# Wider attention units: as many heads as two PSUM banks take, and a unit's transposes issued together

## The chip, the cores and the metric

The kernel runs on one core of one Trainium2 chip. The metric is the device time of one execution in microseconds (us), and the number compared is the median of several runs. A profiled execution is a further one, whose trace the profile is made of. TensorE (PE) multiplies matrices, VectorE (DVE) and ScalarE (ACT) work on rows, GpSimd (POOL) does a few small steps, and SyncE (SP) starts the transfers. Each engine takes its instructions strictly in program order and waits on semaphores for the others.

## What is computed

Two transformer blocks over 512 tokens of width 1024. The first has eight-head attention under a top-k mask, a retention branch and a feed-forward part; the second has native sparse attention (a compressed, a selected and a window branch), gated linear attention and a feed-forward part with a convolution. What matters here is the softmax attention, of which the first block holds one and the second two (selected "s" and window "w"), each with 8 heads of 64:

```python
# first block: one attention, keys chosen by a mask
logits = jnp.einsum('bqhd,bqkhd->bqhk', qb, kg).astype(jnp.float32) * att_scale
logits = jnp.where(valid[:, :, None, :], logits, NEG)
p = jax.nn.softmax(logits, axis=-1).astype(v.dtype)
return jnp.einsum('bqhk,bqkhd->bqhd', p, vg)

# second block: the compressed branch, then two more whose outputs are gated and added
s_cmp = jnp.einsum('bsghd,bngd->bghsn', q, k_cmp)
p_cmp = masked_softmax(s_cmp, cmp_end[None, :] <= pos[:, None])
o_cmp = jnp.einsum('bghsn,bngd->bsghd', p_cmp.astype(dt), v_cmp).reshape(B, S, NSA_HEADS, D)
```

## The kernel before

The 512 tokens are four tiles of 128. The weight products ("dense" here) make up most of the program: every weight is split into a high and a low part (tiles `wh`, `wl`), the activations too (`Hh`, `Hl`), and three matmuls make one product. The loop over a stage's weight chunks and tiles advances in **ticks**; most ticks are six dense matmuls. Class `Weave` runs other work between the ticks: a generator registered with `w.beside(side, every)` goes on by one step, up to its next `yield`, after every tick or every second one. All engines run the same schedule of ticks and yields, each issuing its own part, so the order on each engine is fixed when the program is built. ScalarE and VectorE also split the coming weights (L1176, L1680) in that order.

Attention is such a generator, once per engine. The first block's (`att1`) runs beside the stages `gr0` and `gr1`, one step every second tick; the second block's (`att2`) beside `2nq`, `2gv` and `2gqk`, one step every tick. Its **units** are two heads each: `(i, hp, br)` is query tile i (0 to 3), head pair hp and branch br. Tile i looks at (i+1) x 128 keys. `att1` has 16 units, `att2` 32. One unit passes through four parts, spread over steps u to u+3:

- **scores** (PE, L539): for each of the two heads a product with 64 rows of contraction, q against (i+1) x 128 keys, the first head into bank 4 and the second into bank 5. The two heads lie on rows 0 to 63 and 64 to 127.
- **max** (DVE, L2001): adds the mask and takes the row's extreme, from PSUM into SBUF; **exp** (ACT, L1348) with the row sum; **scale** (DVE, L1708 reciprocal, L1695 `tensor_scalar`), one step later.
- **turn** (PE, L548): i+1 transposes for each head, into bank 6 for the first and bank 3 for the second; ACT copies them out (L1355).
- **values** (PE, L539): for each key block and head a product of 64 columns, accumulated in bank 7 for the whole tile.

In step u TensorE issues: turn of the first head of unit u-2, scores of unit u, turn of the second head of u-2, values of u-3. Scores wait until max of the unit before has read banks 4 and 5. When the last unit of a tile has gone, `att2` adds the compressed branch (eight products, tile `PCT`), for which the generator yields until that branch is ready, and bank 7 is read out.

Beside it in the second block runs `compressed()`, which for each tile makes eight small score products in the same banks 4 and 5 (operands `PRMT`, `ACC`), whose results DVE must read (tile `PRMT`, L1692) before the banks can be used again; transposes of queries and of the linear branch run there too, and `linear()` follows once attention has ended.

Of the kernel before, what the change touches and what calls it, by code (L numbers as in the profile page):

```python
# [5 lines left out]
S, D, P, T = 512, 1024, 128, 4  # L6
# [303 lines left out]
def program(nc, x_in, cst_in, prm_in, bc_in, brow_in, wst, out):  # L310
# [12 lines left out]
    with ctx:  # L323
# [136 lines left out]
        LEAST, SUMS = ST[:, 592:600], ST[:, 600:608]  # L460
# [53 lines left out]
        class Attention:  # L514


            def __init__(self, tag, branches, scr, pt, sbanks, tbanks):
                self.tag, self.scr, self.pt, self.sbanks, self.tbanks = tag, scr, pt, sbanks, tbanks

                self.units = [(i, hp, br) for i in range(T) for hp in range(4) for br in branches]  # L520
                self.first, self.last = branches[0], branches[-1]

# [6 lines left out]
        def tensor_program(e, on):  # L529
# [254 lines left out]
            def attention(a, query, key, value, ready, vready, extra=None):  # L784
                n = len(a.units)

                def turn_part(u, j):
                    i, p = a.units[u][0], 2 * u + j
                    b, src = a.tbanks[p % len(a.tbanks)], a.scr[p % len(a.scr)]
                    turn(b, [src[:, tok(kb)] for kb in range(i + 1)], dve.of((a.tag, "scaled", p)), (a.tag, "turned", p))  # L790
                    free[b] = act.of((a.tag, "pT", p))

                def scores(u):
                    i, hp, br = a.units[u]
                    for r in ready(i, br):
                        on.wait_ge(*r)
                    for b in a.sbanks:
                        claim(b)
                    for j, b in enumerate(a.sbanks):
                        h = 2 * hp + j  # L800
                        mm(bank[b][:, 0:(i + 1) * P], query(i, h), key(br, i, h), True, True).then_inc(*small.mark((a.tag, "score", 2 * u + j)))
                        free[b] = dve.of((a.tag, "max", 2 * u + j))

                def values(u):
                    i, hp, br = a.units[u]
                    first = hp == 0 and br == a.first
# [5 lines left out]
                    for kb in range(i + 1):  # L812
                        for j in (0, 1):
                            o = bank[7][64 * j:64 * j + 64, tok(hp)]
                            x = mm(o, value(br, kb, 2 * hp + j), a.pt[(2 * u + j) % 4][:, tok(kb)], first and kb == 0, False)
                    x.then_inc(*small.mark((a.tag, "value", u)))
                    if hp == 3 and br == a.last:
                        free[7] = dve.of((a.tag, "out", i))

                for u in range(n + 3):  # L820
                    if 2 <= u < n + 2:
                        turn_part(u - 2, 0)
                    if u < n:
                        scores(u)
                    if 2 <= u < n + 2:
                        turn_part(u - 2, 1)
                    if u >= 3:
                        values(u - 3)
                        i, hp, br = a.units[u - 3]
                        if hp == 3 and br == a.last and extra:  # L830
                            yield from extra(i)
                    yield

# [332 lines left out]
        def scalar_program(e, on):  # L1166
# [173 lines left out]
            def attention(a, extra=None):  # L1340
                n = len(a.units)

                def exps(u):
                    i = a.units[u][0]
                    for p in (2 * u, 2 * u + 1):
                        sc, q = a.scr[p % len(a.scr)][:, 0:(i + 1) * P], p % 8
                        on.wait_ge(*dve.of((a.tag, "max", p)))
                        e.activation(sc, sc, ACT.Exp, scale=-1.0, bias=LEAST[:, q:q + 1], accum_out=SUMS[:, q:q + 1]).then_inc(*act.mark((a.tag, "exp", p)))  # L1348

                def turn_part(u, j):  # L1350
                    p, m = 2 * u + j, (a.units[u][0] + 1) * P
# [5 lines left out]
                for u in range(n + 3):  # L1357
# [5 lines left out]
                    if u >= 3:  # L1363
                        i, hp, br = a.units[u - 3]
                        if hp == 3 and br == a.last:
# [4 lines left out]
                    yield  # L1370

# [291 lines left out]
        def vector_program(e, on):  # L1663
# [323 lines left out]
            def attention(a, mask, mready, coef, cready, extra=None):  # L1987
                n = len(a.units)

                def scores(u):  # L1990
                    i = a.units[u][0]
                    m = (i + 1) * P
                    for j in (0, 1):
                        p = 2 * u + j
                        sc = a.scr[p % len(a.scr)][:, 0:m]
                        on.wait_ge(*small.of((a.tag, "score", p)))
                        if p >= len(a.scr):
# [3 lines left out]
                        e.tensor_tensor_reduce(out=sc, in0=bank[a.sbanks[j]][:, 0:m], in1=mask(i), scale=-0.125, scalar=-GONE, op0=ADD, op1=MIN,  # L2001
                                               accum_out=LEAST[:, p % 8:p % 8 + 1]).then_inc(*dve.mark((a.tag, "max", p)))

                def scale(u):
                    i, hp, br = a.units[u]
                    on.wait_ge(*act.of((a.tag, "exp", 2 * u + 1)))
                    pair = SUMS[:, 2 * u % 8:2 * u % 8 + 2]
                    recip(pair, pair)
                    own()
                    if coef:  # L2010
                        on.wait_ge(*cready)
                    for j in (0, 1):
                        p = 2 * u + j
                        sc, r = a.scr[p % len(a.scr)][:, 0:(i + 1) * P], SUMS[:, p % 8:p % 8 + 1]
                        ts(sc, sc, r, coef(i, 2 * hp + j, br) if coef else None, MUL, MUL if coef else None, (a.tag, "scaled", p))

                for u in range(n + 3):
# [4 lines left out]
                    if u >= 3:  # L2022
                        i, hp, br = a.units[u - 3]
                        if hp == 3 and br == a.last:
# [4 lines left out]
                    yield  # L2029

# [321 lines left out]
            def second_attention():  # L2352
                yield
                yield from attention(att2, lambda i: C("cm", (3 - i) * P, (i + 1) * P), lambda i: (s_cst2, 16),
                                     lambda i, h, br: gt[:, i, 3 * h + 1 + "sw".index(br):3 * h + 2 + "sw".index(br)], act.of(("gt",)), add_compressed)
# [316 lines left out]
```

## Time and profile before

| | us |
|---|---|
| median of 3 runs | 1606.05 (1603.98 to 1607.24) |
| the profiled execution's own time | 1602.26 |
| its span | 1600.4 |
| PE busy in the span | 1576.0 (98%) |
| DVE busy | 875.0 (55%) |
| ACT busy | 613.2 (38%) |
| DMA queue q1, share of 16 engines | 29.7% |

Rows of the page and of the trace carry the line, the engine, the operation, output <- inputs, the shape and a count. A float32 matmul of scores, values or compressed scores appears as two records, so "x4" in a timeline row of scores is two products; a transpose and a dense matmul are one record each. Matmuls overlap, so a record's duration is longer than its share of the engine; what a group takes is read as the time from its first start to the next group's first start.

### The profile page before, as it was taken

What the parts mean: (1) busy time and instruction counts of PE and PEld (TensorE: products, weight loads), DVE (VectorE), ACT (ScalarE), POOL (GpSimd) and SP (SyncE); (2) the same over time, 40 slices, a digit from 0 to 9 for tenths busy, and PEclk for the clock granted to TensorE, in tenths of its full rate; (3) what the DMA queues carried; (4) which work ended last, traced back from release to release, by engine and by line L of the source; (5) the groups of instructions that cost most, each with busy time, mean ns of one, the idle gap of its engine ahead of it and who ended that gap; (6) DMA issues with size and microseconds to landing.
All of it is one profiled execution on the core that took longest, in us unless ns stands there. A gap on an engine that the chain in (4) does not pass through costs nothing.

```text
span 1600.4 us, 19799 instructions
## 1 busy us (share of the span) xinstructions
PE 1576.0 (98%) x8019; PEld 1257.9 (79%) x8019; DVE 875.0 (55%) x1604; ACT 613.2 (38%) x1068; POOL 44.3 (3%) x82
## 2 busy tenths in 40 slices
PE   7999999999999999999999999999999999999999
PEld 5777887678888888888888886666768988888887
DVE  6679785655365653232333665676357555555432
ACT  4443334542312432222332454566425434343330
POOL 0000000000000000000000101100010000000000
PEclk9999999999999999999999999999999999999999
DMA  9322121146345334322232142110113232223321
GB/s 389 129 79 93 56 77 54 52 163 221 104 171 171 106 138 152 105 93 94 90 106 92 43 166 74 41 54 14 40 53 117 93 106 92 90 82 105 108 77 53
DMA packets 44883, 165.76 MB, mean 104 GB/s; under 512 B 5108, under 2 KB 5236, under 8 KB 43640
## 3 DMA queue, kind: packets, MB, share of 16 engines
q1 hardware_dynamic: 44792, 164.50, 29.7%
q8 instruction: 63, 1.03, 0.3%
q14 instruction: 28, 0.23, 0.0%
HBM read 162.38 MB, written 2.10 MB: 103 GB/s over the span
## 4 chain that ended last, share of the span: by engine, by line
PE 92%; DVE 5%; ACT 2%; issue 1%; POOL 1%; DMA 0%; SPq 0%; DVEq 0%; ACTq 0%
PE bank L539 87%; PE bank L548 4%; DVE AR L1692 1%; DVE wl L1680 1%; POOL ST L2483 0%; DVE G L1699 0%; DVE X L1692 0%; DVE Hl L1692 0%; ACT wh L1176 0%; ACT AR L1199 0%; DVE CST L1692 0%; ACT AR L1187 0%; DMA CST<-in_cst 0%; DVE ST L1702 0%; DVE AR L1699 0%
## 5 line engine op out<-in xcount | busy, mean ns | idle before, releaser
L539 PE MATMUL bank<-wh,Hh 128*128 128x512 f32 (+1 forms) x1008 | 407.6, 404 | 1.9 <-DVE Hl L1692 1.0
L539 PE MATMUL bank<-wh,Hl 128*128 128x512 f32 (+1 forms) x1008 | 391.6, 389 | 0.0
L539 PE MATMUL bank<-wl,Hh 128*128 128x512 f32 (+1 forms) x1008 | 390.9, 388 | 0.0
L1176 ACT ACTIVATE wh<-raw 128x1024 fp32r<-128x1024 f32 (+1 forms) x195 | 203.6, 1047 | 398.2 <-PE bank L539 386.2
L1680 DVE TENSOR_TENSOR wl<-raw,wh 128x1024 fp32r<-128x1024 f32 (+1 forms) x195 | 234.2, 1208 | 137.1 <-ACT wh L1176 136.1
L539 PEld LDWEIGHTS bank<-wh,Hh 128*128 128x128 f32 x1008 | 189.5, 188 | 60.3 <-issue 24.9
L539 PEld LDWEIGHTS bank<-wh,Hl 128*128 128x128 f32 x1008 | 189.4, 188 | 40.0
L539 PEld LDWEIGHTS bank<-wl,Hh 128*128 128x128 f32 x1008 | 189.8, 188 | 33.9
L539 PE MATMUL bank<-Hh,wh 128*128 128x512 f32 (+2 forms) x504 | 190.2, 377 | 1.0 <-DVE AR L1692 0.7
L539 PE MATMUL bank<-Hl,wh 128*128 128x512 f32 (+2 forms) x504 | 189.4, 376 | 0.0
L539 PE MATMUL bank<-Hh,wl 128*128 128x512 f32 (+2 forms) x504 | 189.4, 376 | 0.0
L539 PEld LDWEIGHTS bank<-Hh,wh 128*128 128x128 f32 (+1 forms) x504 | 94.5, 187 | 18.6 <-DVE AR L1692 0.9
L1692 DVE TENSOR_TENSOR Hl<-AR,Hh 128x512 fp32r<-128x512 f32 x68 | 45.8, 689 | 115.5 <-ACT Hh L1459 109.2
L539 PEld LDWEIGHTS bank<-Hh,wl 128*128 128x128 f32 (+1 forms) x504 | 94.5, 187 | 17.7
L539 PEld LDWEIGHTS bank<-Hl,wh 128*128 128x128 f32 (+1 forms) x504 | 94.5, 187 | 17.6 <-issue 0.2
L548 PEld LDWEIGHTS bank<-CST,AR 128*128 128x128 f32 (+1 forms) x545 | 66.3, 144 | 44.9 <-issue 10.9
L548 PE MATMUL bank<-CST,AR 128*128 128x128 f32 (+1 forms) x545 | 88.8, 285 | 12.0 <-DVE AR L1695 9.0
L539 PE MATMUL bank<-Hh,Ah 128*128 128x512 f32 (+1 forms) x272 | 99.4, 365 | 0.5 <-DVE X L1692 0.5
L539 PE MATMUL bank<-Hh,Al 128*128 128x512 f32 (+1 forms) x272 | 99.0, 364 | 0.0
L539 PE MATMUL bank<-Hl,Ah 128*128 128x512 f32 (+1 forms) x272 | 99.0, 364 | 0.0
L1176 ACT ACTIVATE Ah<-raw 128x1024 fp32r<-128x1024 f32 x46 | 48.6, 1058 | 125.5 <-PE bank L539 119.3
L1699 DVE SCALAR_TENSOR_TENSOR AR<-bank,PRMT,AR 128x511 f32<-128x511 f32 x88 | 63.8, 746 | 56.2 <-ACT AR L1655 54.7
(249 smaller groups left out, 1851.4 us busy)
## 6 DMA issues: line engine op xcount, KB each, us to landing
raw<-in_wst SPq DMA_DIRECT2D x268, 512.0 KB, 3.6
AR<-in_wst SPq DMA_DIRECT2D x8, 1024.0 KB, 11.0
X<-in_x SPq DMA_DIRECT2D x8, 512.0 KB, 4.5
AR<-in_wst SPq DMA_DIRECT2D x5, 512.0 KB, 5.5
out<-X SPq DMA_DIRECT2D x8, 256.0 KB, 2.1
CST<-in_cst SPq DMA_DIRECT2D x1, 1619.0 KB, 11.8
raw<-in_wst SPq DMA_DIRECT2D x4, 296.0 KB, 2.7
BC<-in_bc SPq DMA_DIRECT2D x2, 512.0 KB, 8.2
```

Source lines behind the costliest of these rows:

```text
L539: return e.matmul(o, l, r, start=start, stop=stop, skip_group_check=True)
L548: return e.transpose(o, a, C("ident")[0:n, 0:n])
L1176: e.activation(HI[slot[i]][:, 0:width(i)], raw[:, i % NR, 0:width(i)], ACT.Copy).then_inc(*w_hi.mark(i))
L1680: e.tensor_tensor(LO[slot[i]][:, 0:n], raw[:, i % NR, 0:n], HI[slot[i]][:, 0:n].bitcast(f32), SUB).then_inc(*w_lo.mark(i))
L1692: return e.tensor_tensor(o, a, b, op).then_inc(*dve.mark(*events))
L1699: return e.scalar_tensor_tensor(out=o, in0=a, scalar=s, in1=b, op0=op0, op1=op1).then_inc(*dve.mark(*events))
```

## The change

Banks 4 and 5 hold 512 columns each, and a unit of two heads fills 128 to 512 of them. Now a unit holds as many head pairs as fit: four pairs for tile 0, two for tile 1, one for tiles 2 and 3. `att1` has 1 + 2 + 4 + 4 = 11 units and `att2` twice that, 22. In a unit of several pairs the scores of pair n go to columns n x m on, m being (i+1) x 128; VectorE and ScalarE still do max and exp head by head. The reciprocal is one for the unit; the gate of `att2`, formerly the second scalar of `tensor_scalar`, is multiplied into the reciprocals by one small `tensor_tensor`, and in a unit of several pairs the scaling is one `tensor_tensor` for all the first heads and one for all the second, with the factor broadcast. The generator yields twice after the step of a unit of several pairs. On TensorE a step now is: both turns of u-2, scores of u, values of u-3. `LEAST` and `SUMS` take 16 columns each.

```diff
-                self.units = [(i, hp, br) for i in range(T) for hp in range(4) for br in branches]
+                self.units = [(i, hps, br) for i, sets in enumerate((((0, 1, 2, 3),), ((0, 1), (2, 3)), ((0,), (1,), (2,), (3,)), ((0,), (1,), (2,), (3,))))
+                              for hps in sets for br in branches]
...
+            def ends(self, u):
+                i, hps, br = self.units[u]
+                return hps[-1] == 3 and br == self.last
...
                 def turn_part(u, j):
-                    i, p = a.units[u][0], 2 * u + j
+                    (i, hps, _), p = a.units[u], 2 * u + j
...
-                    turn(b, [src[:, tok(kb)] for kb in range(i + 1)], dve.of((a.tag, "scaled", p)), (a.tag, "turned", p))
+                    turn(b, [src[:, tok(n)] for n in range(len(hps) * (i + 1))], dve.of((a.tag, "scaled", p)), (a.tag, "turned", p))
...
-                    for j, b in enumerate(a.sbanks):
-                        h = 2 * hp + j
-                        mm(bank[b][:, 0:(i + 1) * P], query(i, h), key(br, i, h), True, True).then_inc(*small.mark((a.tag, "score", 2 * u + j)))
-                        free[b] = dve.of((a.tag, "max", 2 * u + j))
+                    for n, hp in enumerate(hps):
+                        for j, b in enumerate(a.sbanks):
+                            x = mm(bank[b][:, n * m:n * m + m], query(i, 2 * hp + j), key(br, i, 2 * hp + j), True, True)
+                            if hp == hps[-1]:
+                                x.then_inc(*small.mark((a.tag, "score", 2 * u + j)))
+                                free[b] = dve.of((a.tag, "max", 2 * u + j))
...
                 for u in range(n + 3):
                     if 2 <= u < n + 2:
                         turn_part(u - 2, 0)
+                        turn_part(u - 2, 1)
                     if u < n:
                         scores(u)
-                    if 2 <= u < n + 2:
-                        turn_part(u - 2, 1)
                     if u >= 3:
                         values(u - 3)
...
+                    yield
+                    if u < n and len(a.units[u][1]) > 1:
+                        yield
...
-                    pair = SUMS[:, 2 * u % 8:2 * u % 8 + 2]
-                    recip(pair, pair)
+                    sums = SUMS[:, a.base[u]:a.base[u] + 2 * n]
+                    recip(sums, sums)
                     own()
                     if coef:
                         on.wait_ge(*cready)
+                        tt(sums, sums, coef(i, br)[:, 2 * hps[0]:2 * hps[0] + 2 * n], MUL)
+                        own()
                     for j in (0, 1):
-                        p = 2 * u + j
-                        sc, r = a.scr[p % len(a.scr)][:, 0:(i + 1) * P], SUMS[:, p % 8:p % 8 + 1]
-                        ts(sc, sc, r, coef(i, 2 * hp + j, br) if coef else None, MUL, MUL if coef else None, (a.tag, "scaled", p))
+                        sc = a.scr[(2 * u + j) % len(a.scr)][:, 0:n * m]
+                        if n == 1:
+                            ts(sc, sc, sums[:, j:j + 1], None, MUL, None, (a.tag, "scaled", 2 * u + j))
+                        else:
+                            s3, r = sc.rearrange("p (n q) -> p n q", n=n), sums.rearrange("p (n c) -> p n c", c=2)[:, :, j]
+                            tt(s3, s3, r.unsqueeze(2).broadcast_to([P, n, m]), MUL, (a.tag, "scaled", 2 * u + j))
```

How the order moves. On TensorE in the first attention, a step of tile 1 before: between the last dense matmul of one tick and the first of the next lie a turn (`CST` is the identity), scores (`X`, `AF`), a turn and values (`AR 64x128`).

```order
L539 MATMUL bank<-wh,Hl 128x512
L548 MATMUL bank<-CST,AR 128x128 x2
L539 MATMUL bank<-X,AF 128x256 x2
L548 MATMUL bank<-CST,AR 128x128 x2
L539 MATMUL bank<-AR 64x128 x2
L539 MATMUL bank<-wh,Hh 128x512
```

On TensorE in the first attention, a step of the change: turns of the last tile-1 unit, scores of a tile-2 unit, values of a tile-1 unit.

```order
L547 MATMUL bank<-wh,Hl 128x512
L556 MATMUL bank<-CST,AR 128x128 x8
L547 MATMUL bank<-X,AF 128x384 x2
L547 MATMUL bank<-BC,AR 64x128 x8
L547 MATMUL bank<-wh,Hh 128x512
```

Eight transposes now stand in one row, where two rows of two stood on either side of the scores, and the values of two pairs in one.

On TensorE in the second attention, the first of the compressed branch's four score groups (`PRMT,ACC`) with the attention step behind it, before (`G,ACC` are scores of the selected branch):

```order
L539 MATMUL bank<-wh,Hl 128x512
L539 MATMUL bank<-PRMT,ACC 128x32 x8
L548 MATMUL bank<-CST,AR 128x128
L539 MATMUL bank<-G,ACC 128x128 x2
L548 MATMUL bank<-CST,AR 128x128
L539 MATMUL bank<-wh,Hh 128x512
```

And the same place on TensorE now (`AR,ACC` are scores of the window branch, all eight heads of tile 0):

```order
L547 MATMUL bank<-wh,Hl 128x512
L547 MATMUL bank<-PRMT,ACC 128x32 x8
L547 MATMUL bank<-AR,ACC 128x128 x8
L547 MATMUL bank<-wh,Hh 128x512
L547 MATMUL bank<-wl,Hh 128x512
```

No turn stands between the compressed scores and the attention scores at this first place; at the other three all of a unit's turns stand there.

## Rows read from the trace of the kernel before

**Rows 1.** Page, busy time of the engines: us, share of the span, instructions.

```profile
PE 1576.0 (98%) x8019; PEld 1257.9 (79%) x8019; DVE 875.0 (55%) x1604; ACT 613.2 (38%) x1068; POOL 44.3 (3%) x82
```

**Rows 2.** Windows: us from:to, length, busy us (count) per engine, granted clock, DMA.

```profile
256.00:346.00 90.00, 90.00 (x534) 64.05 (x533) 55.08 (x146) 48.62 (x119) 0.00 (x0) 1.00 0.23 78
1008.00:1147.00 139.00, 137.37 (x983) 94.53 (x983) 92.64 (x303) 81.73 (x224) 1.90 (x2) 0.99 0.10 35
```

**Rows 3.** Waits of PE, 1000 to 1150 us: total, times, longest.

```profile
PE bank L539 <- DVE PRMT L1692: 1.5, 4, 0.4
```

**Rows 4.** Timeline of PE, a step in tile 1: start, duration, instruction, shape, records.

```profile
284.69 0.39 PE L539 MATMUL bank<-wh,Hl 128*128 128x512 f32 x1
284.92 0.38 PE L548 MATMUL bank<-CST,AR 128*128 128x128 f32 x2
285.23 0.70 PE L539 MATMUL bank<-X,AF 64*128 64x256 f32 x4
285.86 0.44 PE L548 MATMUL bank<-CST,AR 128*128 128x128 f32 x2
286.23 0.66 PE L539 MATMUL bank<-BC,AR 128*64 128x128 f32 x8
286.82 0.50 PE L539 MATMUL bank<-wh,Hh 128*128 128x512 f32 x1
287.15 0.39 PE L539 MATMUL bank<-wl,Hh 128*128 128x512 f32 x1
```

**Rows 5.** Timeline of PE, scores of 512 keys in tile 3.

```profile
1112.16 1.13 PE L539 MATMUL bank<-AR,ACC 64*128 64x512 f32 x4
1113.22 0.66 PE L548 MATMUL bank<-CST,AR 128*128 128x128 f32 x4
```

**Rows 6.** Timeline of PE, a step without scores: both turns, then values.

```profile
333.53 1.03 PE L548 MATMUL bank<-CST,AR 128*128 128x128 f32 x8
334.50 1.09 PE L539 MATMUL bank<-AR 128*64 128x128 f32 x16
335.52 0.50 PE L539 MATMUL bank<-wh,Hh 128*128 128x512 f32 x1
```

**Rows 7.** Timeline of PE in the linear branch: products of two shapes in turn.

```profile
1154.49 0.38 PE L539 MATMUL bank<-AR,CST 128*128 128x128 f32 x2
1154.80 0.43 PE L539 MATMUL bank<-AR 64*64 64x128 f32 x2
1155.16 0.49 PE L539 MATMUL bank<-AR,CST 128*128 128x128 f32 x2
1155.58 0.43 PE L539 MATMUL bank<-AR 64*64 64x128 f32 x2
```

**Rows 8.** Timeline of PE, compressed scores before attention scores, with the wait.

```profile
1024.63 1.08 PE L539 MATMUL bank<-PRMT,ACC 64*128 64x32 f32 x16
1025.64 0.33 PE L548 MATMUL bank<-CST,AR 128*128 128x128 f32 x1
1026.39 0.49 PE L539 MATMUL bank<-G,ACC 64*128 64x128 f32 x4 [0.42 <-DVE PRMT L1692]
```

**Rows 9.** Windows, the stretch behind it.

```profile
1028.00:1030.00 2.00, 2.00 (x6) 1.23 (x5) 1.93 (x8) 1.19 (x5) 0.00 (x0) 0.50 0.00 0
```

**Rows 10.** Timeline of DVE in tile 0: scale, max, and a 512-wide tensor_tensor.

```profile
1016.93 0.60 DVE L1695 TENSOR_SCALAR AR<-AR,ST 128x128 f32<-128x128 f32 x2
1017.45 0.28 DVE L2001 CUSTOM_DVE_ANT_0 AR<-bank,CST 128x128 f32<-128x128 f32 x1
...
1017.66 0.28 DVE L2001 CUSTOM_DVE_ANT_0 AR<-bank,CST 128x128 f32<-128x128 f32 x1
...
1020.69 0.69 DVE L1692 TENSOR_TENSOR AR<-AR,ST 128x512 f32<-128x512 f32 x1
```

**Rows 11.** Timeline of ACT in tile 0: one exp.

```profile
1017.78 0.40 ACT L1348 ACTIVATE AR<-AR,ST 128x128 f32<-128x128 f32 x1 [0.45 <-DVE ST L2001]
```

**Rows 12.** Windows, tiles 0 and 1 of the second attention.

```profile
1008.00:1074.00 66.00, 64.37 (x430) 43.50 (x430) 50.60 (x189) 37.29 (x122) 1.90 (x2) 0.97 0.12 41
```

More of the change, by code:

```diff
@@ L811, in values @@
                         on.wait_ge(*r)
[L812 to L815, printed above, removed]
+                    for n, hp in enumerate(hps):
+                        for kb in range(i + 1):
+                            for j in (0, 1):
+                                o = bank[7][64 * j:64 * j + 64, tok(hp)]
+                                x = mm(o, value(br, kb, 2 * hp + j), a.pt[(2 * u + j) % 4][:, tok(n * (i + 1) + kb)], first and n == 0 and kb == 0, False)
                     x.then_inc(*small.mark((a.tag, "value", u)))
-                    if hp == 3 and br == a.last:
+                    if a.ends(u):
                         free[7] = dve.of((a.tag, "out", i))
@@ L822, in attention @@
                         turn_part(u - 2, 0)
+                        turn_part(u - 2, 1)
                     if u < n:
                         scores(u)
-                    if 2 <= u < n + 2:
-                        turn_part(u - 2, 1)
                     if u >= 3:
                         values(u - 3)
-                        i, hp, br = a.units[u - 3]
-                        if hp == 3 and br == a.last and extra:
-                            yield from extra(i)
+                        if a.ends(u - 3) and extra:
+                            yield from extra(a.units[u - 3][0])
                     yield
+                    if u < n and len(a.units[u][1]) > 1:
+                        yield
             w.beside(attention(att1, lambda i, h: qaT[64 * (h % 2):64 * (h % 2) + 64, h // 2, tok(i)],
@@ L1363, in attention @@
                     if u >= 3:
-                        i, hp, br = a.units[u - 3]
-                        if hp == 3 and br == a.last:
+                        i = a.units[u - 3][0]
+                        if a.ends(u - 3):
                             if extra:
@@ L1370, in attention @@
                     yield
+                    if u < n and len(a.units[u][1]) > 1:
+                        yield
             w.beside(attention(att1), 2)
@@ L1990, in scores @@
                 def scores(u):
-                    i = a.units[u][0]
+                    i, hps, _ = a.units[u]
                     m = (i + 1) * P
@@ L2022, in attention @@
                     if u >= 3:
-                        i, hp, br = a.units[u - 3]
-                        if hp == 3 and br == a.last:
+                        i = a.units[u - 3][0]
+                        if a.ends(u - 3):
                             if extra:
@@ L2029, in attention @@
                     yield
+                    if u < n and len(a.units[u][1]) > 1:
+                        yield
             w.beside(attention(att1, lambda i: MASK[i] if i else C("cm", 384, 128), lambda i: dve.of(("mask", i)) if i else (s_cst2, 16), None, None), 2)
```

37 lines of the change are left out of this document (23 added, 14 removed).

## The prediction

> **What bounds the kernel now.** I read the page's busy times first: PE is busy for 1576.0 of 1600.4 us, DVE for 875.0 [rows 1]. A change helps only by what it takes from PE's own queue. Next, the windows over the two attentions: in the first, 256 to 346 us, PE has no gap at all; in the second, 1008 to 1147 us, it has 1.6 us of gaps in 139 [rows 2], and nearly all of that is four waits of at most 0.42 us for VectorE to read the compressed scores out of banks 4 and 5 [rows 3, 8]. So there is almost no waiting to remove. But "busy" is not "at peak": a record's duration covers fill and drain. So I went to the timeline and measured from start to start.
>
> **What a step costs on PE.** The step in tile 1 [rows 4] takes 0.31 (two transposes), 0.63 (scores over 256 keys), 0.37 (two transposes) and 0.59 (eight records of values), and the first dense matmul behind it takes 0.33 where a dense one in its run takes 0.23. Each part is a stream plus a fixed price:
> - Turns: eight transposes in one go take 0.97 [rows 6], two take 0.31, so 0.11 each, and 0.09 fixed behind dense work. Behind scores, two take 0.37, so 0.15 fixed.
> - Scores: 256 keys 0.63, 512 keys 1.06 [rows 4, 5], so 0.215 per 128 keys and 0.20 fixed.
> - Values: eight records 0.59, sixteen 1.02 [rows 4, 6], so 0.054 a record and 0.16 fixed.
> - Way back to dense work: 0.33 - 0.23 = 0.10.
>
> The fixed prices add up to 0.09 + 0.20 + 0.15 + 0.16 + 0.10 = 0.70 us a full step. With 16 units the first attention has 19 steps, of which 13 are full (the first three and the last three lack a part); with 32 the second has 35, of which 29 are full. 42 x 0.70 = 29.4 us of fixed prices.
>
> **What the change makes of it.** The streams stay: as many products, transposes and records as before. Two things shrink.
>
> Fewer steps: 11 and 22 units give 8 and 19 full steps, 27 for 42. That a unit of several pairs pays each fixed price once, I take from the compressed scores, which are eight products on eight different weights, on the same alternating rows, and take 1.01 us for 16 records [rows 8]: 0.2 and 0.05 a record. And from the eight transposes into two banks in 0.97 [rows 6].
>
> Both turns together: one turn loses its fixed price of 0.15, and values now stand behind scores, a neighbourhood that the trace does not have. Call what it adds to values x. A turn behind scores costs 0.06 more than behind dense work (0.37 to 0.31); in the linear branch a product of full shape takes 0.42 behind one of quarter shape and 0.31 behind dense work [rows 7], 0.11 more. The ends I keep are 0, if any neighbour is alike to values (I see no reason for less, since the drain of scores has to end somewhere), and 0.22, twice the dearer row. I take 0.09, between the two rows. A full step then costs 0.09 + 0.20 + 0.16 + 0.09 + 0.10 = 0.64, and 27 of them 17.3 us: **12.1 us less** (14.5 with x = 0, 8.6 with x = 0.22). The partial steps at both ends stay as many and cost about the same.
>
> Given back, part one: other small groups that used to share a tick with attention now stand alone, since a unit of several pairs leaves its second tick empty and the second attention ends earlier. In the new order I count seven: the transposes of compressed probabilities twice, of queries once, of the linear branch four times. Each pays entry and exit, 0.09 + 0.10: **1.3 us more**.
>
> Given back, part two: the waits for VectorE, 1.7 us in all before. From compressed to attention scores the chain over VectorE takes 1026.39 - 1024.63 = 1.76 us [rows 8]. At the first of the four places no turn stands between now, so 1.76 - 1.01 = 0.75 is waited there. At the other three stand all of a unit's turns: 1.01 + 0.97 is more than 1.76, and that wait goes. What is late next is VectorE's queue. Tile 0 and 1 of the second attention now pass in fewer ticks, with the same VectorE work of others beside them. I followed the queues from the first wide unit. Eight maxes at 0.21, eight exps at 0.40 [rows 10, 11] and two scale passes of about 0.65 make the way from scores to scaled about 7.5 us, and 9.9 us lie between the scores of unit 0 and its turn (two dense stretches of twelve at 0.23, the compressed group and unit 1's scores): no wait. At the second compressed group VectorE still has a unit's scale, four maxes and the normalisation of a query tile ahead (two passes like the 0.69 one [rows 10] and smaller ones): I get 0.4 for the banks and 1.1 us for the next scores. From there on it keeps up by 2 us and more. First place 0.75, the copy ahead of it 0.15, second place 1.5: 2.4 against 1.7, **0.7 us more**. Its ends are -1.6 (every wait gone) and +3 (1.1 us at three further places).
>
> At nothing I cost the rest. One `tensor_tensor` of 512 at 0.69 for the wide units replaces four `tensor_scalar` of 128, two of which take 0.52 [rows 10], so VectorE gains; in tiles 2 and 3 of the second attention the gate's own small multiply adds some 0.2 us to each of 16 units, between max and turn, with more than 2 us of slack; without that cover it would be 0.2 a unit, 3.2 us. The stages of the first attention tick at every second tick, with twice the room. The last values of the first attention, which a transfer on SP's queue awaits, come no later.
>
> The Trainium skill, "TensorEngine Tiling (Array Packing)", section "Key Properties", says that changing the tiling mode, not just the tile, drains the engine. The trace agrees that a change costs 0.1 to 0.2 us; by that rule alone the 0.70 would sit on four changes a step and leave three, which is the second rival below.
>
> **Sum.** 12.1 - 1.3 - 0.7 = 10.1 us. The profiled execution took 1602.26 us, so it would take 1592.2; the median of the runs stands 3.8 us above it. Forecast of the median: **1596.0 us**.
>
> **Rivals.**
> - *Each further pair pays again.* If in a wide unit the scores and values of every pair pay their fixed 0.20 and 0.16, the 15 pairs that join others give 5.4 us back: 1606.05 - 4.7 = 1601.4. For it: no row has several pairs of scores over 128 or more keys. Against: the 1.01 us of the compressed scores.
> - *Only changes of shape are paid.* The step goes full, half rows, full, half columns, full: four changes for 0.70, 0.175 each. Three changes make 0.53 a step, 27 x 0.53 = 14.3, 15.1 less, and 13.1 after what is given back: 1593.0. Against: two transposes behind dense work, with no change of shape, still pay 0.09.
> - *The clock falls for longer.* Between 1028 and 1030 us the granted clock is 0.50, the lower level of 1.2 GHz, and six matmuls begin in those 2 us, where at 0.23 us it would be nearly nine [rows 9]; it follows the compressed group with its small products and the wait [rows 8]. A mean of 0.97 over the 66 us of these tiles [rows 12] is 4 us at the lower level, which by the starts missed costs about 1.6 us now. Four such dips, one after each compressed group, would cost 4.8 us more: 1600.8. Against: two of the four waits go. The Trainium skill, "TensorE: Matmul & The Clock Gate", section "What's actually happening", lets the clock follow how busy the array has recently been; by that, waits at these places could be paid twice.
> - *VectorE becomes the bound* (the slower side). Place: the turns of the six wide units of the second attention, which wait for the scaling. By my count the tightest has 2.5 us of slack. If the chain of eight exps and maxes is 5 us longer than I think, 2.5 us are waited six times, 15 us, with 10.1 gained: 1611. It decides from 1.7 us of wait per wide unit on. For it: VectorE is busy for 50.6 of the 66 us of tiles 0 and 1 [rows 12]. Of that the new order keeps some 44 there (2.8 less of scaling, the rest a unit of tile 2 and a weight split that fall outside), and PE's own work for the stretch, 14 dense ticks of 1.37 and some 32 us of groups, is 51 us. Against: today it keeps up with waits of 0.42.
>
> **How the numbers follow.** Forecast 0.60; further pairs pay 0.10; only changes of shape 0.12; clock 0.10; VectorE 0.08. What a measurement of this kernel can tell from no change is about 0.2%, 3.2 us. The forecast and the shape rival are faster; of the pair and clock rivals three quarters; of the VectorE rival a fifth; the rest of each is the same, or slower for most of VectorE's. Faster 0.88, same 0.07, slower 0.05. The range: x alone gives 1592.5 to 1599.5, waits -2.3 to +2.3 more, the shape rival 1593.0, the clock rival 1600.8 and the pair rival 1601.4: 1590.5 to 1602.0.
>
> **What would show it.** PE waits between 1000 and 1140 us of 2 to 3 us; a wide unit of tile 0 whose scores take 1.06; values behind scores at 0.59 + x for eight records; DVE's count down, PE's unchanged at 8019. PE waits of over 10 us for the scaled rows, or a granted clock of 0.5 over tens of us, would make the forecast wrong.

## The result, and the profile after

The changed kernel takes **1591.92 us** in the median of 6 runs (1591.13 to 1597.39), the kernel before 1605.71 in the median of 6 (1601.37 to 1607.24). The ratio is 0.9924, with an interval of 0.9906 to 0.9942: faster, by more than the 0.2% that can be told, and 4.1 us below my forecast of 1596.0, inside its range. One further execution of the kernel before, of 3992.09 us, taken beside e9, is an outlier that no run explains and is in no comparison. The profiled execution took 1591.81 us, 10.4 less than the profiled one of before, where my sum had said 10.1. That this is nearly right is partly luck, as the terms show.

The page's row of PE, the windows that answer to [rows 2, 9, 12], and the waits of PE between 995 and 1140 us that answer to [rows 3]:

```profile
PE 1561.9 (98%) x8019; PEld 1259.0 (79%) x8019; DVE 870.8 (55%) x1581; ACT 606.3 (38%) x1038; POOL 44.7 (3%) x82
```

```profile
256.00:346.00 90.00, 90.00 (x556) 68.51 (x555) 55.08 (x131) 48.61 (x112) 0.00 (x0) 1.00 0.24 83
1008.00:1147.00 139.00, 135.10 (x1015) 99.69 (x1014) 87.55 (x283) 76.31 (x199) 1.91 (x2) 0.98 0.09 32
1008.00:1074.00 66.00, 62.10 (x484) 47.14 (x484) 50.27 (x175) 38.41 (x115) 1.91 (x2) 0.95 0.10 35
1028.00:1030.00 2.00, 2.00 (x10) 1.38 (x7) 1.93 (x8) 2.00 (x9) 0.00 (x0) 0.50 0.00 0
```

```profile
PE bank L547 <- DVE PRMT L1710: 1.6, 2, 0.9
PE bank L547 <- DVE ST L2020: 1.3, 1, 1.3
PE bank L556 <- DVE PRMT L1710: 1.0, 1, 1.0
```

PE's busy time falls by 14.1 us with the same 8019 instructions. In 90 us of the first attention 556 of them start instead of 534: the same work in a denser row. The second attention gives something back: waits are 3.9 us, where they were 1.7 and I had said 2.4, and the granted clock stays longer at its lower level of 1.2 GHz (0.50). The windows around that fall, before and then after:

```profile
1020.00:1030.00 10.00, 9.58 (x61) 6.64 (x57) 8.43 (x35) 4.62 (x19) 0.00 (x0) 0.89 0.00 0
1030.00:1040.00 10.00, 10.00 (x58) 6.44 (x57) 6.78 (x30) 5.66 (x20) 0.00 (x0) 0.94 0.01 2
...
1020.00:1030.00 10.00, 7.83 (x54) 5.88 (x53) 9.69 (x36) 5.87 (x20) 0.00 (x0) 0.70 0.01 2
1030.00:1040.00 10.00, 10.00 (x78) 7.94 (x76) 6.18 (x23) 5.30 (x14) 0.00 (x0) 0.96 0.00 1
```

What the clock took can be summed from them: 10 us times what it lacks of 1. Before that is 1.1 + 0.6 = 1.7 us, now 3.0 + 0.4 = 3.4 us, that is 3.4 and 6.8 us at the lower level. In both profiles the clock is 1.00 in every other window of 10 us.

A full step of tile 2, and the wide units of tile 0 in both attentions (four pairs in one unit), on PE:

```profile
1062.24 0.40 PE L547 MATMUL bank<-wh,Hl 128*128 128x512 f32 x1
1062.47 0.82 PE L556 MATMUL bank<-CST,AR 128*128 128x128 f32 x6
1063.22 0.92 PE L547 MATMUL bank<-AR,ACC 64*128 64x384 f32 x4
1064.07 0.88 PE L547 MATMUL bank<-AR 128*64 128x128 f32 x12
1064.88 0.50 PE L547 MATMUL bank<-wh,Hh 128*128 128x512 f32 x1
1065.21 0.40 PE L547 MATMUL bank<-wl,Hh 128*128 128x512 f32 x1
...
258.26 1.16 PE L547 MATMUL bank<-X,AF 64*128 64x128 f32 x16
259.35 0.50 PE L547 MATMUL bank<-wh,Hh 128*128 128x512 f32 x1
...
1009.87 1.16 PE L547 MATMUL bank<-AR,ACC 64*128 64x128 f32 x16 [0.68 <-DVE PRMT L1710]
1010.96 0.50 PE L547 MATMUL bank<-wh,Hh 128*128 128x512 f32 x1
```

From start to start: turns 0.75 for six transposes (0.66 of stream at 0.11 and 0.09 fixed), scores 0.85 for 384 keys (0.645 and 0.20), values 0.81 for twelve records (0.65 and 0.16), dense again 0.33 (0.10 over 0.23). So values behind scores cost the same 0.16 as values behind a turn: **x is 0**, not 0.09, and a full step pays 0.55, not 0.64. And the wide units take 1.09: one stream of four times 128 keys and one fixed price, as forecast.

### The profile page after: what moved, and what is told of

Its sections match the earlier page's. It is cut to its first block, busy times and chain, and to the rows that moved or that the text cites. A ratio compares the mean times of both kernels' runs of the same rounds, so it can differ in the third digit from the quotient of the medians.

```text
span 1590.0 us, 19712 instructions
## 1 busy us (share of the span) xinstructions
PE 1561.9 (98%) x8019; PEld 1259.0 (79%) x8019; DVE 870.8 (55%) x1581; ACT 606.3 (38%) x1038; POOL 44.7 (3%) x82
## 4 chain that ended last, share of the span: by engine, by line
PE 90%; DVE 5%; ACT 2%; issue 1%; DMA 1%; POOL 1%; SPq 0%; DVEq 0%; ACTq 0%
PE bank L547 87%; PE bank L556 4%; DVE AR L1710 1%; DMA raw<-in_wst 1%; DVE wl L1698 1%; POOL ST L2511 0%; DVE G L1717 0%; DVE X L1710 0%; DVE Hl L1710 0%; DVE ST L1720 0%; ACT wh L1188 0%; DVE ST L1710 0%; ACT AR L1211 0%; DVE CST L1710 0%; DVE AR L2020 0%
## 5 line engine op out<-in xcount | busy, mean ns | idle before, releaser
L556 PE MATMUL bank<-CST,AR 128*128 128x128 f32 (+1 forms) x545 | 77.7, 279 | 12.6 <-DVE AR L1713 9.6
```

Of the source, the lines that this page charges most:

```text
L556: return e.transpose(o, a, C("ident")[0:n, 0:n])
```

## Where the waits come from

```profile
1018.52 0.44 PE L556 MATMUL bank<-CST,PRMT 128*128 128x128 f32 x2 [1.00 <-DVE PRMT L1710]
1021.63 1.08 PE L547 MATMUL bank<-PRMT,ACC 64*128 64x32 f32 x16 [1.29 <-DVE ST L2020]
1022.65 1.09 PE L556 MATMUL bank<-CST,AR 128*128 128x128 f32 x8
1024.62 2.08 PE L547 MATMUL bank<-AR,ACC 64*128 64x256 f32 x8 [0.88 <-DVE PRMT L1710]
1026.63 1.97 PE L547 MATMUL bank<-AR 128*64 128x128 f32 x16
```

Those are PE's rows, without the dense ones. From the third wait on the granted clock is 0.50, and the scores take 2.08 and the values 1.97 where 1.13 and 1.09 are usual. The next rows are ACT's and then DVE's, in the same stretch:

```profile
1013.16 0.40 ACT L1363 ACTIVATE AR<-AR,ST 128x128 f32<-128x128 f32 x1 [3.46 <-DVE ST L2020]
...
1016.25 0.40 ACT L1541 ACTIVATE PRMT<-PRMT 128x256 f32<-128x256 f32 x1
```

```profile
1016.69 0.42 DVE L1720 TENSOR_REDUCE ST<-PRMT 128x8 f32<-128x256 f32 x1 [2.72 <-ACT PRMT L1541]
...
1021.41 0.69 DVE L1710 TENSOR_TENSOR AR<-AR,ST 128x512 f32<-128x512 f32 x1
...
1024.00 0.48 DVE L1710 TENSOR_TENSOR PRMT<-bank,CST 128x128 f32<-128x128 f32 x2
```

On ACT the exp of the compressed scores (L1541) stands behind the eight exps of the wide unit, and VectorE, which needs it for the compressed probabilities, idles for 2.72 us. All that stands behind it on VectorE is late by as much: the probabilities that PE transposes at 1018.52, and the maxes that free the banks awaited at 1021.63. The wait of 0.88 has its own cause: VectorE reads the compressed scores out only after it has normalised a query tile (1021.41 to 1023.66). In my forecast I followed VectorE's queue, which found the 0.88 (as 1.1), and put ACT's eight exps on the way from scores to scaled, but never asked what ACT had queued behind them.

## Experiments

Executions of one kernel differ in mean granted clock, and their spans follow it. In batch 1 the kernel before has spans of 1599.3 to 1599.8 us at a mean clock of 1.000, 1601.6 to 1603.0 at 0.998, 1605.4 to 1605.7 at 0.996: about 1.6 us per 0.001. So beside each ratio I compare spans at one clock; the clock is given to 0.001, so this is good to about 1 us.

The last column is finer, though it rests on the one profiled execution of each kernel. It takes the time from the first scores of the first attention (257.40 us before, 258.26 in the changed kernel) to the end, less what the clock took, and says how much shorter that is than the 1341.3 us of before. In brackets stands what the step prices (0.70 with a turn on either side of the scores or between scores and values, 0.55 with both turns first) and the waits make of it. The changed kernel, measured twice, gives 13.0 and 13.3, e3 14.6 and 14.5. All brackets are within 1.3 us.

| kernel | median us | ratio to before, interval | waits of PE 995 to 1140 | span at a clock | gain without the clock |
|---|---|---|---|---|---|
| the change | 1591.92 | 0.9924, 0.9906 to 0.9942 | 3.9 | 1589.3 to 1590.0 at 0.998 | 13.0 (12.2) |
| before | 1604.24 | | 1.7 | 1601.6 to 1603.0 at 0.998 | |
| e0 the change again | 1592.11 | 0.9926, 0.9913 to 0.9940 | 3.6 | 1588.9 to 1589.5 at 0.998 | 13.3 (12.5) |
| e1 turns together | 1597.14 | 0.9968, 0.9953 to 0.9982 | 0.8 | 1593.7 to 1594.9 at 0.999 | 6.6 (7.0) |
| e2 wide units only | 1597.98 | 0.9965, 0.9952 to 0.9977 | 4.5 | 1595.9 to 1596.3 at 0.997 | 7.8 (7.7) |
| e3 compressed exp first | 1591.90 | 0.9917, 0.9902 to 0.9931 | 2.1 | 1587.8 at 0.998 | 14.6 (14.0) |
| e4 scores first | 1597.54 | 0.9964, 0.9952 to 0.9976 | 6.1 | 1595.1 to 1595.7 at 0.998 | 7.3 (6.1) |
| e5 wide in the first attention | 1594.85 | 0.9943, 0.9931 to 0.9956 | 1.2 | 1592.7 to 1592.9 at 0.998 | 9.1 (9.6) |
| e6 tile 0 in two units | 1599.25 | 0.9966, 0.9954 to 0.9979 | 4.7 | 1593.5 to 1594.9 at 0.997 | 9.8 (9.9) |
| e8 queries later | 1597.85 | 0.9966, 0.9953 to 0.9978 | 5.4 | 1596.0 to 1597.6 at 0.994 | 11.5 (10.7) |
| e3 again | 1588.17 | 0.9901, 0.9883 to 0.9918 | 2.1 | 1587.5 to 1587.8 at 0.998 | 14.5 (14.0) |
| e9 query earlier | 1587.13 | 0.9901, 0.9882 to 0.9919 | 1.2 | 1585.0 to 1586.4 at 0.999 | 15.9 (14.9) |

e1 to e4 and the line "before" are one batch, e0 and e5 to e8 a second (before 1604.01), e3 again and e9 a third (before 1604.17).

### e1, e2, e4: what the fixed price hangs on

e1 is the kernel before with its second turn moved ahead of the scores:

```diff
                     if 2 <= u < n + 2:
                         turn_part(u - 2, 0)
+                        turn_part(u - 2, 1)
                     if u < n:
                         scores(u)
-                    if 2 <= u < n + 2:
-                        turn_part(u - 2, 1)
```

> The kernel before with one edit: on TensorE both turns of a unit come ahead of the scores; units stay two heads each (42 full steps). Theory A (a fixed price is paid at each change of tile shape, about 0.18 us; turns next to dense work pay none): three changes instead of four in 42 steps, 42 x 0.15 = 6.3 us less, 1599.4 against 1605.7. Theory B (the recorded prediction: values behind scores cost 0.09 more): 42 x 0.06 = 2.5 us less, 1603.2. In the trace a full step with 384 keys and 12 value records should be 2.51 us (A) or 2.60 (B) where it was 2.66, and waits of PE should stay near 1.7 us.

A step of e1 on PE:

```profile
1076.61 0.81 PE L548 MATMUL bank<-CST,AR 128*128 128x128 f32 x6
1077.36 0.92 PE L539 MATMUL bank<-G,ACC 64*128 64x384 f32 x4
1078.20 0.88 PE L539 MATMUL bank<-BC,AR 128*64 128x128 f32 x12
1079.01 0.50 PE L539 MATMUL bank<-wh,Hh 128*128 128x512 f32 x1
1079.35 0.39 PE L539 MATMUL bank<-wl,Hh 128*128 128x512 f32 x1
```

0.75 + 0.84 + 0.81 and 0.11 for the way back is 2.51 us. The same step (384 keys, twelve records of values, three transposes on either side of the scores) starts at 1080.72 us in the trace of before and takes 0.42 + 0.85 + 0.47 + 0.81 + 0.11 = 2.66. That is Theory A's 2.51, not B's 2.60. Each of 42 steps saves 0.14 or 0.15, some 6.1 us; waits fall by 0.9, 7.0 in all. The median is 7.1 below that of before. At a clock of 0.999 four of e1's six spans are 1594.3 to 1594.4, where before has 1600.4 (profiled) and 1601.8: 6.0 to 7.5 less.

e2 is the changed kernel with the old order (turn, scores, turn, values), so wide units alone.

```diff
                         turn_part(u - 2, 0)
-                        turn_part(u - 2, 1)
                     if u < n:
                         scores(u)
+                    if 2 <= u < n + 2:
+                        turn_part(u - 2, 1)
```

> The changed kernel with the old order in a step: turn, scores, turn, values. Units stay wide (27 full steps). Theory A: a fourth change of shape comes back in 27 steps, 27 x 0.15 = 4.1 us slower than the changed kernel, 1597.6 if that is 1593.5. Theory B: 27 x 0.06 = 1.6 us slower, 1595.1. The waits around the compressed scores should stay near 3.9 us under both, since they come from VectorE's and ScalarE's queues.

Fifteen full steps fewer at the old 0.70 are 10.5 us, and 2.8 more of waits leave 7.7; at 0.997 the spans lie 7.9 us below the 1603.7 to 1604.4 of before. So both halves do what was said of them.

e4 is the changed kernel with the scores first, then both turns, then values:

```diff
+                    if u < n:
+                        scores(u)
                     if 2 <= u < n + 2:
                         turn_part(u - 2, 0)
                         turn_part(u - 2, 1)
-                    if u < n:
-                        scores(u)
```

> The changed kernel with the order scores, both turns, values in a step. The turns are still one group of one shape, but stand between scores and values, so the shape changes four times a step instead of three. Theory A (changes of shape are paid): as dear as the old order, 27 x 0.15 = 4 us slower than the changed kernel, 1597.5. Theory G (groups are paid, and a group of turns is saved by joining the two): no slower, 1593.5.

It has as few groups as the changed kernel, but four changes of tile shape (dense, half rows, full, half columns, dense) where that has three. Its step on PE:

```profile
1078.67 0.39 PE L547 MATMUL bank<-wh,Hl 128*128 128x512 f32 x1
1078.98 0.92 PE L547 MATMUL bank<-G,ACC 64*128 64x384 f32 x4
1079.83 0.88 PE L556 MATMUL bank<-CST,AR 128*128 128x128 f32 x6
1080.64 0.88 PE L547 MATMUL bank<-BC,AR 128*64 128x128 f32 x12
1081.44 0.50 PE L547 MATMUL bank<-wh,Hh 128*128 128x512 f32 x1
1081.78 0.40 PE L547 MATMUL bank<-wl,Hh 128*128 128x512 f32 x1
```

0.31 instead of 0.23 into the scores, 0.85, 0.81, 0.80, and 0.34 out: 2.65 us with the extras of the dense rows, as in the kernel before. Joining the turns thus saves nothing by itself; it saves where it takes a change of shape away. Full steps pay 0.70 with four changes and 0.55 with three, 0.18 each. e4's median of 1597.54 meets Theory A's 1597.5 partly by luck: it is 5.6 us above the change's, and only 4.1 of that are the 27 steps. PE also waits 6.1 us there instead of 3.9, which no theory had.

### e0, e5, e6: what the second attention gives back

e0 is the changed kernel once more, beside e5 to e8.

> The changed kernel itself once more, beside the variants of this group and on their chip, to compare them with. Both theories expect its ratio to the kernel before near 0.992. Theory K (the runs of one kernel differ by how long the granted clock stays low in them): over its runs, span and granted clock lie on one line, 1.6 us of span for each 0.001 of clock.

It repeats the result: 0.9926 against 0.9924, waits of 3.6, and a granted clock of 0.76 between 1020 and 1030 us. Its spans of 1588.9 to 1589.5 at a clock of 0.998 and 1590.3 to 1591.7 at 0.997 are in line with Theory K's 1.6 us per 0.001.

e5 keeps units of one pair in the second attention:

```diff
-  self.units = [(i, hps, br) for i, sets in enumerate((((0, 1, 2, 3),), ((0, 1), (2, 3)), ...))
+  self.units = [(i, hps, br) for i, sets in enumerate((((0, 1, 2, 3),), ((0, 1), (2, 3)), ...)
+                                                      if tag == "a1" else (((0,), (1,), (2,), (3,)),) * T)
```

> Wide units in the first attention only; the second keeps two heads a unit (16 and 32 units become 11 and 32), turns together in both. Theory A (0.55 us of fixed prices per full step, nothing given back in the first attention): 5 steps fewer than with turns alone, 5 x 0.55 = 2.8 us faster than that kernel (1597.1 median there), 1594.4, with waits as there (0.8 us) and nearly no fall of the clock. Theory W' (the wide units of the second attention give most of their 5.5 us back by waits and the clock): then this kernel is within 2 us of the whole change. If they give nothing back it should be about 5 us slower than the whole change.

Ten steps at 0.55 come back, 5.5 us, and the waits fall from 3.9 to 1.2: 2.8 us slower is what that makes, and at 0.998 it is 3.6 slower than e0. The wide units of the second attention gain, though half of their gain goes into waits. That lies between Theory W' (within 2 us) and no loss at all (5 us).

e6 splits tile 0 into two units of two pairs, which halves VectorE's and ACT's burst:

```diff
-  (((0, 1, 2, 3),), ((0, 1), (2, 3)), ...
+  (((0, 1), (2, 3)), ((0, 1), (2, 3)), ...
```

> The changed kernel with tile 0 in two units of two pairs instead of one of four (12 and 24 units; 30 full steps). Blocks of exps in front of the compressed exp are four long instead of eight. Theory W (the eight exps in a row make the waits): 3 x 0.55 = 1.7 us more of fixed prices, but the waits at the second compressed group fall from 3.2 us to under 1.5 and the clock stays up more often, so within 1 us of the change on the median. Theory D (VectorE's amount of work is what counts): waits fall too, since the stretch gets two more ticks, to under 1 us. Theory N (the waits have another cause): waits as before and 1.7 us slower.

A miss for every theory: the waits do not fall but are 4.7 (nearest to Theory N, which had them as before), and the median is 7.1 us above e0's, not 1 or 1.7. Three of its five executions ran at a clock of 0.994 or 0.995. The longest wait now stands later:

```profile
1051.17 1.13 PE L547 MATMUL bank<-AR,ACC 64*128 64x256 f32 x8 [1.63 <-DVE PRMT L1710]
```

Ahead of reading those compressed scores (from 1050.54 on) VectorE waits 1.94 us for ACT and then has a job of 0.69 us and a weight split of 1.22 us. Three more steps (1.7 us) and 0.8 more of waits make 2.5 of the 3.3 us that it is slower than e0 at 0.997; the rest stays open.

### e3, e8, e9: the queues

e3 is the changed kernel with the compressed exps one tick earlier on ACT, ahead of the wide unit's exps instead of behind:

```diff
-                for _ in range(11):
+                for _ in range(10):
                     yield
...
-                    pct.add(i)
                     yield
+                    pct.add(i)
```

> The changed kernel with one edit on ScalarE: the compressed branch's exp goes one tick earlier in program order, so ahead of the eight exps of a wide unit instead of behind them. Theory W (the waits behind the first compressed group come from that exp standing behind eight others, and the fall of the clock from the waits): the waits of 1.00 and 1.29 us go and the 0.88 shrinks to under 0.3, PE waits between 1000 and 1140 us 3.9 to about 1 us, the granted clock stays at 1.00 there, 5 to 6 us faster than the changed kernel, about 1588. Theory D (VectorE has too much work in this stretch, whatever the order): the transposes' wait goes but the same time is waited at the next group, gain under 1 us, about 1593. Theory C (the clock falls because of the many small products, not of the waits): gain of the waits alone, about 3 us, and 0.5 of clock still for some microseconds.

The wait of the transposes is gone, that of 1.3 is 0.5, and that of 0.88 stays, which Theory W had expected under 0.3:

```profile
PE bank L547 <- DVE PRMT L1710: 1.6, 2, 0.9
PE bank L547 <- DVE ST L2020: 0.5, 1, 0.5
```

In the first batch the median was 1591.90, not told from the change, with clocks down to 0.996; in the third it was 1588.17. At a clock of 0.998 all three of its executions have spans of 1587.5 to 1587.8, where the change has 1588.9 to 1590.0: 1.1 to 2.5 less, for 1.8 us less waiting. At 0.997 it is 0.1 to 1.6 less (1590.1, where the change has 1590.2 to 1591.7). Without the clock its two profiles are 1.1 to 1.7 us ahead of the change's two.

e8 is e3 with the query tile one tick or two later on VectorE, PE and ACT, so that its normalisation no longer stands ahead of the compressed scores:

```diff
-                    w.after((4, 4, 10, 10)[t], scale)
+                    w.after((4, 4, 12, 10)[t], scale)
...
-                    w.after((7, 7, 13, 14)[t], ...)
+                    w.after((7, 7, 14, 14)[t], ...)
```

> The changed kernel with two edits: the compressed branch's exp one tick earlier on ScalarE, and the normalisation of query tile 2 on VectorE two ticks later (its transposes and copy one tick later), so that it stands behind the reading of the second compressed scores. Theory W (each wait comes from what stands ahead of the awaited instruction in its engine's queue): of the waits between 995 and 1140 us only the first, 0.7 us, stays and perhaps 0.3 at the second group; 3 us less than in the change, 1 to 1.5 less than with the exp alone. With less waiting the clock falls less often: median 1588 against 1592. Theory C (the clock falls with the small products, whatever the waits): waits go, but the runs spread over the same clocks, 0.994 to 0.999, and the median gains 3 us at most.

The wait of 0.88 did go, but I had put the query's transposes and those of the compressed probabilities, which share a bank, into one tick, and PE waited 4.22 us for ACT to empty it. The median is 1597.85, 10 us above the 1588 expected. PE's row there, and two windows:

```profile
1037.69 0.41 PE L556 MATMUL bank<-CST,PRMT 128*128 128x128 f32 x2 [4.22 <-ACT ACC L1223]
```

```profile
1020.00:1030.00 10.00, 9.54 (x86) 7.73 (x88) 8.76 (x30) 6.77 (x22) 0.00 (x0) 1.00 0.01 2
1040.00:1050.00 10.00, 10.00 (x59) 7.74 (x58) 6.51 (x21) 3.47 (x11) 0.00 (x0) 0.58 0.03 6
```

As an experiment on the clock it is the clearest: the second compressed group, at 1020, runs at full clock with its waits down to 0.48, and the fall comes behind the 4.22 us of waiting instead, between 1038 and 1050. In this profile the fall follows the wait, not the group with its small products and the eight transposes behind it, which are the same at 1020 as in the changed kernel.

e9 is e3 with that normalisation earlier instead, into the time in which VectorE waits for ACT's `wh`:

```diff
-                    w.after((4, 4, 10, 10)[t], scale)
+                    w.after((4, 4, 4, 10)[t], scale)
```

> The changed kernel with the compressed exp of e3, and VectorE's normalisation of query tile 2 (about 2.2 us of 128x512 work) moved into VectorE's own idle time of 3.2 us at 1001.7 to 1004.9, so that it no longer stands ahead of the reading of compressed scores. If the waits of TensorE in the second attention are VectorE's queue order, the two waits at the second compressed group (0.5 and 0.9 in e3) go, 1.0 or less is left between 995 and 1140, and the time falls below e3's by 1.2 to 1.6: 1589.5 to 1591, with a step of the granted clock there in fewer executions. If the waits only move on to the next reading (VectorE is simply full there), 2 us of waits stay and the time is e3's 1591.9. If taking the normalisation early delays the split of the weights or the first maxima, TensorE waits for these at about 1006 and the time is 1593.

> e3 once more, beside e9 on one chip: 1591 to 1592 in the median, with 2.1 us of waits between 995 and 1140. Any difference to e9 is read against this run.

VectorE's rows of e9, and PE's waits:

```profile
1007.07 0.69 DVE L1710 TENSOR_TENSOR AR<-AR,ST 128x512 f32<-128x512 f32 x1
...
1009.11 0.29 DVE L1710 TENSOR_TENSOR AR<-ST 128x128 f32<-128x128 f32 x1
1010.38 1.22 DVE L1698 TENSOR_TENSOR wl<-raw,wh 128x1024 fp32r<-128x1024 f32 x1 [0.98 <-ACT wh L1188]
```

```profile
PE bank L547 <- DVE PRMT L1710: 0.7, 1, 0.7
PE bank L547 <- DVE ST L2020: 0.5, 1, 0.5
```

The normalisation fits whole into idle time: the split of the weights behind it still waits 0.98 us for ACT. PE's wait of 0.9 is gone and nothing is late in its place. The ratios of e9 and e3 are alike (0.9901), so the runs do not tell them apart; at a clock of 0.999 e9's spans are 1585.0, 1585.2, 1585.3 and 1586.4, e3's of the same batch 1585.8, 1586.2 and 1586.3, 0.6 less in the mean with ranges that overlap. Only the profiles tell them apart: without the clock e9's is 1.3 to 1.4 us ahead of e3's two, which differ by 0.2. Two waits, of 0.7 and 0.5, are left. Both medians came out lower than expected (e3 again 1588.17, not 1591 to 1592), since e3's executions ran at 0.998 and 0.999 here. With a median of 1587.13 e9 has the lowest median here, 1.0% below the kernel before in its batch; the changed kernel, in other batches, stood 0.74 to 0.76% below.

## Why the prediction was right, and where its terms were not

- **Steps: 12.1 forecast, 14.5 by the measured prices.** Step counts and the single price for a wide unit hold. The mis-sized term is x, what values add behind scores: 0.09 forecast, 0 in every full step of the changed kernel and of e1. 29.4 - 27 x 0.55 = 14.5, which the forecast named as the end for x = 0. In the first attention, where nothing waits, the time from its first scores to the first of the second attention falls from 750.6 us (257.40 to 1008.05) to 745.6 (258.26 to 1003.90); that is 5.0, where 13 x 0.70 - 8 x 0.55 is 4.7 and x = 0.09 would have made 4.0.
- **Why x is 0.** The rival by changes of shape was nearest: it said 0.53 a step, and e1 and e4 show that a change is what is paid. I had two rows for a price of neighbourhood, a turn behind scores and a product behind quarter tiles [rows 4, 7], and took a value between them. But those are changes between full shape and part shape, and values behind scores are one change as well, and it was already counted in the 0.16. The rule of the Trainium skill that I quoted ("TensorEngine Tiling (Array Packing)", "Key Properties": a change of tiling mode drains the engine) agrees with the prices here, 0.18 us a change; that it is a drain that is paid, no run shows.
- **Small groups alone in a tick: 1.3 forecast, 0.1 measured.** Two transposes between dense matmuls in the changed kernel:

```profile
1129.71 0.38 PE L556 MATMUL bank<-CST,AR 128*128 128x128 f32 x2
1129.85 0.48 PE L547 MATMUL bank<-wh,Hh 128*128 128x512 f32 x1
1130.16 0.39 PE L547 MATMUL bank<-wl,Hh 128*128 128x512 f32 x1
```

  From 1129.71 to 1130.16 are 0.45 us; less 0.23 for the dense matmul that is 0.22, the bare stream of two transposes. They have the same shape as dense work and pay nothing; only the first of the seven, at 1018.52, costs 0.06 more. I had charged the entry price of 0.09, which a step shows at its turn, to the turn; it belongs to the change behind it.
- **Waits: 0.7 more forecast, 2.2 more measured.** The first place and the query normalisation (0.75 and 1.1 forecast, 0.68 and 0.88 measured) were right. What failed is "I followed the queues": I followed VectorE's and not ACT's, and missed the transposes' wait of 1.00 and 0.9 of the 1.29. e3 shows ACT's order to be the cause: with the compressed exp earlier the 1.00 is gone and the 1.29 is 0.51, near the 0.4 that I had.
- **The clock: nothing forecast, 1.7 us measured.** It took 3.4 us where it had taken 1.7. The rival of the longer fall had the direction, at a third of its size.
- **The sum.** 14.5 - 0.1 - 2.2 = 12.2, less 1.7 for the clock is 10.5; the two profiles differ by 10.4. My 10.1 came out near by 3.6 us of gain that I did not see and 3.2 us of loss that I did not see. That even 10.5 meets 10.4 is in part chance. By place: 5.0 less in the first attention; in the second, from its first scores to the first group of the linear branch behind it, 139.9 us (1008.05 to 1147.99) become 133.7 (1003.90 to 1137.59), which is 8.0 less without the clock, where the terms make 7.6; and 452.4 us behind it in both. Against that the changed kernel's profile comes to its first attention 0.9 us later, where nothing was changed (and its repeat e0 another 0.4 later). 5.0 + 8.0 - 1.7 - 0.9 is 10.4.
- **The 4.1 us by which the forecast missed** are thus 0.3 in the sum and 3.8 in the step from the profiled execution to the median. I took that the changed kernel's median would stand 3.8 us above its profile as before's did; it stood 0.1 above. Before's profile was one of its executions at high clock (0.999); its median of 1605.71 is what executions at 0.997 take in batch 1 (1605.5 to 1606.2).
- **The range.** Its low end has a slip: x = 0 gives 1606.05 - 12.5 = 1593.5, not 1592.5, and less 2.3 of waits that is 1591.2, not 1590.5. The 1591.92 measured is still inside, but close to that end.
- **Rivals that fell.** Each further pair pays again: the wide units' 1.09 us. VectorE becomes the bound: the longest wait is 1.3 us, and between 995 and 1140 us PE never waits for scaled rows (e6 has one such wait, 0.47 us).

**Left open.** Which executions have a fall of the clock, and how long. In the profiles a fall at 1020 to 1040 us is there with waits of 1.7 (before), 3.6, 3.9, 4.5, 4.7 and 6.1 us, and not there with 0.8, 1.2, 1.2, 2.1 and 2.1 (e1, e5, e9, e3 twice). Before breaks that order. Nor is a wait enough: every profile has a wait of PE of 2.5 to 2.6 us near 990 us, ahead of the second attention. In five of the twelve profiles (e0, e1, e3, e8, e9) the clock falls there and takes 1.7 us, in seven it does not, and the changed kernel and its repeat e0 are on different sides. e9's profiled execution, the slowest of its five, also lost 3.4 us between 10 and 30 us, as e3 again did, and 1.7 us at 500. What the runs show is a tendency, not a threshold.

## What to carry to other kernels

Count the changes of tile shape on TensorE, not the groups: work of the shape that stands beside it is free to enter and leave, and reordering so that full, half-row and half-column products each stand once per step saved 0.15 us a step, while joining groups without saving a change (e4) gave nothing. When a unit of work is made wider, its burst on every engine gets longer: follow the small urgent instruction that stands behind that burst on each engine's queue, ScalarE's too, and move it ahead (e3) or put the long job into a time in which the engine is idle anyway (e9). And set a sum made from one profiled execution against the clock of that execution before it is carried over to a median.

## What the runs showed of the hardware that I had not expected

- A change of tile shape costs 0.18 us on TensorE in the mean (0.70 for four in the kernel before and in e4, 0.55 for three in the changed kernel and in e1), and half rows to half columns counts as one change, not two.
- Two or four transposes between dense matmuls cost 0.11 us each and nothing besides (0.22 us at 1129.71 and 0.44 us at 1045.60 in the changed kernel).
- With waits of 1.00, 1.29 and 0.88 us within 7 us the granted clock fell to 0.50 for 6.8 us, and scores took 2.08 instead of 1.13 us; after one wait of 4.22 us it fell likewise (0.58 over the 10 us from 1040). A wait of 2.5 us near 990 us was followed by a fall in five profiles of twelve.
